# Two hybrid blocks in one kernel: the recurrent pairs and their filler as 64x64 quarters, with "identity minus product" on VectorE

## The reference

```python
def wkv7_scan(r, w, k, v, kk, a, reverse):
    def step(state, inp):
        r_t, w_t, k_t, v_t, kk_t, a_t = inp
        sa = jnp.einsum('bhij,bhj->bhi', state, -kk_t)
        state = (state * w_t[:, :, None, :] + sa[..., None] * (kk_t * a_t)[:, :, None, :]
                 + v_t[..., None] * k_t[:, :, None, :])
        return state, jnp.einsum('bhij,bhj->bhi', state, r_t)
...
    y = direction(0, False) + direction(1, True)      # 8 heads of 64 channels
...
    branch = jnp.einsum('bsnc,ncd->bsnd', ys, w_branch)
    gates = jax.nn.sigmoid(gl.reshape(b, s, N_BRANCH, D_MODEL) + b_gate)
    merged = jnp.sum(gates * branch, axis=2)
```

## Time and profile before

| | |
|---|---|
| median of three runs | 2548.95 us (2546.47 to 2549.86) |
| profiled execution | 2548.45 us, span 2546.7 us |
| granted clock of TensorE, mean | 0.998 |
| PE busy in the span | 2484.2 us, 98% |
| DVE, ACT, POOL busy | 1439.2, 527.6, 316.1 us |

### The profile page before, as it was taken

One profiled execution on the slowest core, in us unless ns is written; L12 is line 12 of the kernel. 1 busy time (PEld: TensorE's weight loads), 2 busy tenths in 40 slices (PEclk: granted clock), 3 DMA queues, 4 the chain that ended last, 5 costly groups with the idle time before them and its releaser, 6 DMA issues. The chain is left out here.

```text
span 2546.7 us, 38463 instructions
## 1 busy us (share of the span) xinstructions
PE 2484.2 (98%) x15968; PEld 1905.6 (75%) x15968; DVE 1439.2 (57%) x2688; ACT 527.6 (21%) x1249; POOL 316.1 (12%) x367
## 2 busy tenths in 40 slices
PE   8999999999999999999999999999999999999998
PEld 7887886854788788685477747888886666666997
DVE  1576655855157655573357735555334488854775
ACT  1342220100134222010014910000003243411000
POOL 2002102110100210221000000000000155410110
PEclk9999999999999999999999999999999999999999
DMA  7331125987433212598632022222222534334553
GB/s 269 116 116 63 57 81 170 303 292 256 147 116 117 68 52 84 179 306 289 239 125 67 2 66 71 96 83 75 91 87 69 165 101 135 121 102 146 167 173 107
DMA packets 253603, 341.80 MB, mean 134 GB/s; under 512 B 7252, under 2 KB 179412, under 8 KB 253304
## 3 DMA queue, kind: packets, MB, share of 16 engines
q1 hardware_dynamic: 241632, 311.71, 37.4%
q10 hardware_dynamic: 8920, 17.67, 2.1%
q0 software_dynamic: 2880, 9.96, 1.0%
HBM read 338.13 MB, written 1.19 MB: 133 GB/s over the span
## 5 line engine op out<-in xcount | busy, mean ns | idle before, releaser
L1058 PE MATMUL PS<-MEM 128*128 128x256 f32 (+1 forms) x2632 | 447.9, 332 | 2.6 <-ACT MEM L1515 1.2
L1058 PEld LDWEIGHTS PS<-MEM 128*128 128x128 f32 x2632 | 406.3, 190 | 43.8 <-issue 1.9
L416 PE MATMUL PS<-MEM 128*128 128x256 f32 x1632 | 356.0, 379 | 0.0
L1474 ACT ACTIVATE MEM<-PS 128x256 f32<-128x256 f32 (+4 forms) x405 | 162.0, 429 | 907.8 <-PE PS L416 221.1
L416 PEld LDWEIGHTS PS<-MEM 128*128 128x128 f32 x1632 | 308.6, 190 | 42.5 <-issue 1.3
L462 PE MATMUL PS<-MEM 128*128 128x512 f32 x608 | 265.4, 597 | 9.1 <-DMA MEM<-w_down 4.3
L2094 DVE SCALAR_TENSOR_TENSOR MEM<-MEM 128x512 f32<-128x512 f32 x280 | 214.4, 798 | 53.7 <-DMA MEM<-ada_w 48.0
L462 PEld LDWEIGHTS PS<-MEM 128*128 128x128 f32 x608 | 115.3, 191 | 155.3 <-issue 141.2
L3038 POOL TENSOR_TENSOR MEM<-MEM 128x1 f32<-128x1 f32 (+1 forms) x34 | 21.6, 637 | 1269.4 <-DVE MEM L2040 812.1
L696 PE MATMUL PS<-MEM 128*128 128x256 f32 x768 | 178.3, 384 | 0.0
L1371 PE MATMUL PS<-MEM 128*128 128x512 f32 (+1 forms) x512 | 171.5, 488 | 0.0
(11 more groups left out here) (384 smaller groups left out, 3259.8 us busy)
## 6 DMA issues: line engine op xcount, KB each, us to landing
MEM<-w_in SPq DMA_DIRECT2D x54, 1024.0 KB, 5.4
MEM<-ada_w SPq DMA_DIRECT2D x48, 1024.0 KB, 7.5
MEM<-w_up SPq DMA_DIRECT2D x32, 1024.0 KB, 5.4
MEM<-w_down SPq DMA_DIRECT2D x32, 1024.0 KB, 5.1
MEM<-ssm_w_in SPq DMA_DIRECT2D x24, 1024.0 KB, 5.4
MEM<-ffn_gate SPq DMA_DIRECT2D x22, 1024.0 KB, 5.3
MEM<-ffn_up SPq DMA_DIRECT2D x22, 1024.0 KB, 5.4
MEM<-ffn_down SPq DMA_DIRECT2D x20, 1024.0 KB, 5.1
```

The source lines that it names most:

```text
L416: ins = pe.matmul(bank[:, 0:T], W[:, k, c * P:(c + 1) * P], XT[:, k, :], start=k == 0, stop=k == KT - 1)
L1058: ins = pe.matmul(out, left[:, k, :], right[:, k, :], start=k == 0, stop=k == 3)
L1474: act.activation(out, view(b), func, **kw).then_inc(S("bank_read_by_act"), 1)
```

## The change

- Every product of the stage but the transposed keys becomes 64x64 (rows x columns of weights). `scores` splits its columns; the right side, the solve and the outputs are split by row half into a first and a second (and third) part, since the second half of the rows adds into the same bank after the first is done, with a semaphore (`row_step`) between them. Quarters of triangular matrices that are zero are left out.
- Filler in this stage runs as pairs of tiles: a step is four 64x64 products of 256 columns over two banks; the first half of a pair's steps takes one row half for each bank, the second the other, with a semaphore (`half_summed`) between.
- VectorE writes identity minus Z instead of ScalarE's copy; X times that is the new X, so ScalarE copies both following products (VectorE one of them at level 5), and VectorE's subtractions go.
- The slots are 2 or 4 steps with the same counts in each pair, their sums end with pairs of tiles; FILL_DECAY is 12 tiles, not 10, and the stage has 112 steps, not 120.
- VectorE reads both states of a pair before both outputs.

```diff
-FILL_LORA, FILL_DECAY, FILL_MEAN, FILL_VAR = 4, 10, 1, 5
+FILL_LORA, FILL_DECAY, FILL_MEAN, FILL_VAR = 4, 12, 1, 5
-FILL_SLOT = {"mask": (4, 0, 0, 0), "begin": (10, 0, 0, 0),
-             ("z", 1): (2, 4, 4, 4), ("z", 2): (0, 0, 0, 0), ("z", 3): (0, 0, 0, 0), ("z", 4): (0, 0, 0, 0), ("z", 5): (4, 4, 4, 4),
-             ("x", 1): (0, 0, 0, 0), ("x", 2): (0, 4, 4, 0), ("x", 3): (0, 0, 0, 0), ("x", 4): (0, 4, 4, 4), ("x", 5): (4, 4, 4, 4),
-             "W": (4, 4, 4, 4), "XO": (2, 2, 2, 4), "sa": (2, 4, 4, 4)}
+FILL_SLOT = {"mask": (4, 0, 0, 0), "begin": (12, 0, 0, 0),
+             ("z", 1): (2,) * 4, ("x", 1): (0,) * 4, ("z", 2): (2,) * 4, ("x", 2): (2,) * 4, ("z", 3): (2,) * 4, ("x", 3): (0,) * 4,
+             ("z", 4): (2,) * 4, ("x", 4): (2,) * 4, ("z", 5): (2,) * 4, ("x", 5): (2,) * 4, "W": (4,) * 4, "XO": (2,) * 4, "sa": (2,) * 4}
...
+                    banks = [bank_for(key, NBANK - 2 + j) for j, key in enumerate(keys)]
+                    for turn in range(2):
+                        if turn:
+                            pe.wait_ge(S("half_summed"), halves[0])
+                        for k in range(nk):
+                            for j, b in enumerate(banks):
+                                r = HB * (j ^ turn)
+                                for o in (0, HB):
+                                    ins = pe.matmul(PS[o:o + HB, b, 0:T], W[r:r + HB, k, (c + j) * P + o:(c + j) * P + o + HB], src[r:r + HB, k, :],
+                                                    start=turn == 0 and k == 0, stop=turn == 1 and k == nk - 1)
...
-                            ins = pe.matmul(banks[half][:, 256 * j:256 * j + 256], BK[pb:pb + 64, d, ct, c, part, :], rhs, start=True, stop=True)
+                            for o in (0, HB):
+                                ins = pe.matmul(banks[half][o:o + HB, 256 * j:256 * j + 256], BK[pb:pb + 64, d, ct, c, part, o:o + HB], rhs, start=True, stop=True)
...
-                        if m in (3, 4):
-                            right_side(gs[m - 3])
                         if m == LEVELS - 1:
                             for g in follow:
                                 keys_flipped(g)
                         slot(pair, ("z", m))
+                        if m == 4:
+                            right_second(gs)
...
+                        if m == 3:
+                            right_first(gs)
                         slot(pair, ("x", m))
                     cross_left(gs)
                     slot(pair, "W")
                     cross_right(gs)
+                    solve_first(gs)
                     slot(pair, "XO")
-                    for g in gs:
-                        solve(g)
+                    solve_second(gs)
+                    outputs_first(gs)
                     slot(pair, "sa")
-                    for g in gs:
-                        outputs(g)
+                    outputs_second(gs)
+                    outputs_third(gs)
...
+                def finer(g):
+
+                    if m < LEVELS - 1:
+                        copy(("dx", l, g, m), flat(UC[g % 2][:, :, :]), lambda b: b[:, 0:256])
+                    elif g % 2 == 0:
+                        b = filled(act, "act", ("dx", l, g, m))
+                        bv = b[:, 0:256].rearrange("p (i n) -> p i n", i=4)
+                        act.activation(AB[g % 4][0:HB, :, 0:HB], bv[0:HB, :, :], ACT.Copy)
+                        act.activation(AB[g % 4][HB:P, :, HB:P], bv[HB:P, :, :], ACT.Copy).then_inc(S("bank_read_by_act"), 1)
...
-                        for g in gs:
-                            copy(("Z", l, g, m), flat(ZI[g % 2][:, :, :]), lambda b: b[:, 0:256])
...
                         slot(("z", m))
+                        if m == 4:
+                            for g in gs:
+                                copy(("rh", l, g), flat(RH[g % 2][:, :, :]), lambda b: b[:, 0:256], scale=-1.0)
+                        for step in (finer_turned, finer) if m == LEVELS - 1 else (finer, finer_turned):
+                            for g in gs:
+                                step(g)
                         slot(("x", m))
...
+                def level_left(g):
+
+                    b = filled(dve, "dve", ("Z", l, g, m))
+                    read(dve.tensor_tensor(ZI[g % 2][:, :, :], eye, b[:, 0:256].rearrange("p (i n) -> p i n", i=4), ALU.subtract))
...
+                        for g in gs:
+                            level_left(g)
                         slot(("z", m))
-                        for step in (finer_turned, finer) if m == LEVELS - 1 else (finer, finer_turned):
-                            for g in gs:
-                                step(g)
+                        if m == LEVELS - 1:
+                            last_diagonal(gs[1])
                         if m in (1, 2):
                             masked("sk", AK, gs[m - 1])
```

More of the change, by code:

```diff
@@ L691, in gate_tiles @@
                         W = a_slab(w_in[l], O_G + D * n + 256 * s)
[L692 to L703, removed]
+                        work = pair_of_tiles([("gl", l, n, 2 * s + c) for c in range(2)], "act", W, 0, XT, KT)
+                        yield from shut(work, 2)
                 def branch_tiles(n, Y):
@@ L708, in branch_tiles, with shut @@
                         W = b_slab(w_branch[l, n], 0, 512 * s)
[L709 to L720, removed]
+                        yield from pair_of_tiles([("br", l, n, 4 * s + c) for c in range(2)], "dve", W, 0, Y, 4)
+                        work = pair_of_tiles([("br", l, n, 4 * s + c) for c in (2, 3)], "dve", W, 2, Y, 4)
+                        yield from shut(work, 2)
+                def shut(work, tiles):
+                    for step in work:
+                        tiles -= step
+                        if tiles == 0:
+                            close_slab()
+                        yield step
                 def gate_work():
@@ L811, in four_blocks @@
                 def four_blocks(gs, keys, by, left, right, halves=(0, HB)):
-                    banks = [take(key, by) for key in keys]
+                    banks = [take(key, who) for key, who in zip(keys, by)]
                     for i in range(4):
@@ L828, in level_z @@
                             emptied(pe, ("dx", l, g, m - 1))
-                    four_blocks(gs, [("Z", l, g, m) for g in gs], "act", lambda g: UM[g % 2][:, m % 2, :, :], lambda g: UC[g % 2])
+                    four_blocks(gs, [("Z", l, g, m) for g in gs], ("dve", "dve"), lambda g: UM[g % 2][:, m % 2, :, :], lambda g: UC[g % 2])
                 def level_x(gs, m):
@@ L872, in cross_right @@
                                 done(ins)
[L874 to L891, removed]
-                                done(ins)
@@ L894, in solve @@
[L894 to L898, removed]
-                    for i in range(4):
[L900 to L917, removed]
-                        ins = pe.matmul(o[i], VTK[:, c, 64 * h:64 * h + 64], AK[i2][:, i, P:2 * P], start=False, stop=wave == 0 and i >= 2)
-                    if wave == 1:
-                        for i, ct, pb, h in inst:
-                            ins = pe.matmul(o[i], ST[pb:pb + 64, d, ct, :], KR[pb:pb + 64, d, ct, c, 1, :], start=False, stop=i >= 2)
-                    done(ins)
@@ new lines, in solve_first @@
+                def solve_first(gs):
+                    for g in gs:
+                        emptied(pe, ("rh", l, g))
+                    open_banks("sa", gs)
+                    for i in range(4):
+                        for g in gs:
+                            for o in (0, HB):
+                                ins = pe.matmul(PS[o:o + HB, opened["sa", g], i * HB:(i + 1) * HB], AB[g % 4][o:o + HB, i, o:o + HB], RH[g % 2][o:o + HB, i, :],
+                                                start=i == 0, stop=i == 3 and o == HB * (g % 2))
+                            if i == 3:
+                                rows_stepped(ins)
@@ new lines, in solve_second @@
+                def solve_second(gs):
+                    for g in gs:
+                        emptied(pe, ("XO", l, g))
+                    other_rows()
+                    for i in range(4):
+                        for g in gs:
+                            f = HB * (g % 2)
+                            r, b = HB - f, opened["sa", g]
+                            ins = pe.matmul(PS[r:r + HB, b, i * HB:(i + 1) * HB], AB[g % 4][f:f + HB, i, r:r + HB], RH[g % 2][f:f + HB, i, :],
+                                            start=False, stop=i == 3)
+                            if i == 3:
+                                numbered(("sa", l, g), "act", b)
+                                done(ins)
@@ new lines, in outputs_first @@
+                def outputs_first(gs):
+                    open_banks("y", gs)
+                    for i in range(4):
+                        for g in gs:
+                            d, c, wave, inst = instances(g)
+                            _, ct, pb, h = inst[i]
+                            f = HB * d
```

(4 more changed lines are left out.)

178 lines of the change are left out of this document (137 added, 41 removed).

## The result

The changed kernel takes 2557.01 us (median of 8 runs, 2552.95 to 2559.38), the kernel before 2549.06 (median of 8 runs in the same comparison; one disturbed run of them, 2891.09, is left out of the ratio). The ratio is 1.0032, 95% interval 1.0023 to 1.0042. It is slower by 0.3%, where 2520 and "faster" were forecast. The profiled execution took 2556.92 us with a span of 2555.1 and a mean granted clock of 0.994.

What follows compares the result with a forecast made beforehand. TensorE, busy 98%, was taken as the bound, with shape changes hidden in "busy". A layer's stage: 3.5 + 10.4 + 112.5 + 14.8 + 1.4 + 1.3 = 143.9 against 158.3; two layers save 28.8, giving 2520 us, range 2499 to 2542.

Steps and rivals of the forecast that it cites:

- Rest: What remains of a layer's stage: 1.4 us for gaps in instruction supply and 1.3 us for the end.
- Theory B: Rival explanation in the experiments: quarters, changes of shape or new waits on VectorE and ScalarE cost more than forecast; no chance given.
- Head: From first scores to first level product: 10.4 us instead of 11.15, as VectorE's queue loses a branch tile.
- steps moved: Eight filler steps (two branch tiles) move ahead of the scores to the decay filler: 3.5 us a layer.
- price of a filler step: Four 64x64 products of 256 columns, four passes at once, take 0.435 us, as one whole product did.
- no loss at a change of shape: With 64x64 products nearly throughout the stage, 110 changes a layer at about 0.16 us, some 17 us, go, all but two round trips.
- The rival in which quarters don't run four at once: Filler passes take turns or pay their weight loads, so the kernel is slower, 2572 or 2604 us; chance 0.06.
- the rule on weight loads: Contrary rule: a load overlaps matmuls in flight only when its row group differs, making a filler step 0.71 us.
- Work and waits of the pairs: TensorE's work in a layer's four pairs, 112.5 us, and its waits there, 14.8 us.
- Supply: Gaps in TensorE's instruction supply, between nothing and 3 us a layer, taken as 1.4.
- The swap of evictions: First product's eviction to VectorE, the two others to ScalarE: no price by itself, both engines answering in 1.1 us.
- I am wrong if ... gaps with no releaser appear by the dozen: Sign against the forecast in the profile after: many TensorE idle gaps that nothing in the profile releases.

Runs made afterwards that it cites:

- whole_filler: The changed kernel with the filler of the pairs as whole 128x128 products again, in the same slots; 2552.18 us, ratio 1.0012.
- slab_pieces: The changed kernel with each weight slab of the stage sent as 8 or 4 DMAs, each held until two more PSUM banks are filled; 2532.05 us, ratio 0.9931.
- pieces_at_once: The changed kernel with the stage's weight slabs sent in 8 or 4 pieces, without waits between the pieces; 2540.6 us, ratio 0.9957.
- slabs_twice: The changed kernel with each weight slab of the stage sent twice, first to a place in DRAM that nothing reads; 2567.79 us, ratio 1.0074.
- pieces_old_evictions: The changed kernel with slabs in pieces and the old evictions: ScalarE copies the first product, VectorE subtracts the two that follow; 2535.69 us, ratio 0.9949.

## Why the prediction was wrong

The step that failed is *Rest*: "Instruction supply ... Bounds: nothing, or a gap in every pair and some (3); I take 1.4." It measured 16.2 and 13.1 us a layer, and the half clock behind it came on top. I had sized it by how often a gap might come, at the 0.3 of the one gap in the earlier trace rows. What sets its length is how late the fetch is, and that was to be read from q8 and q1 in the trace of before: there too no instruction packet comes while a slab runs (271.8 to 275.6: 1021 packets of q1 and none of q8; the next 0.8 us have one). Before, what TensorE had in hand was nearly always enough to bridge that. The number of fetches was to be forecast too: at 250 matmuls and weight loads to a packet, 5120 more are 20 more packets. With 128, 138 and 148 packets (kernel before, whole_filler, changed kernel) the waits without a releaser sum to 0.9, 15.9 and 29.3 us. That the quarters use up sooner what TensorE has in hand fits this; by itself it was not tested, as shapes and slots change along with the count.

The three kernels that move the slabs alone, beside the changed one, account for the loss. Waits and clock are those of the traced execution, so its time stands beside the median. The price of the half clock is an upper bound: 1.7 us for each 3.4 us at 0.50, as the filler block shows (1.77 against 0.86).

| | median, us | traced, us | waits without a releaser, both layers | at half clock in the stages, us |
|---|---|---|---|---|
| slab_pieces | 2532.05 | 2532.66 | 11.6 | 0 |
| pieces_at_once | 2540.6 | 2544.48 | 16.2 | 10.2 |
| changed kernel | 2557.01 | 2556.92 | 29.3 | 20.4 |
| slabs_twice | 2567.79 | 2568.43 | 34.8 | 30.6 |

From slab_pieces to the changed kernel: 17.7 of waits and up to 10.2 of clock, 27.9 for 24.3 between the traced executions; slabs_twice 23.2 and 15.3, 38.5 for 35.8; pieces_at_once 4.6 and 5.1, 9.7 for 11.8, of which a further 3.4 us at half clock outside the stages can hold 1.7. Theory B is not needed for this difference.

The other steps, by slab_pieces, where the supply disturbs least:

- *Head, steps moved, price of a filler step, no loss at a change of shape*: as forecast (in the changed kernel 10.46; the stage starts 3.85 later; 0.43; 0.47). The rival in which quarters don't run four at once is out. So is the rule on weight loads from the Trainium skill ("TensorE: Matmul & The Clock Gate", Part 3), for these products, at 256 columns too: a step takes 0.43, not 0.71.
- *Work and waits of the pairs*: 112.5 + 14.8 = 127.3 forecast. The stage of 146.4 less head 10.5, supply 6.0 and end 1.2 leaves 128.7. The sum came out by luck, as two errors cancel: the trace puts only 5.5 of it down to waits on VectorE and ScalarE, so the work is some 10 longer than I counted block by block, and the waits some 9 shorter. Short waits that the trace doesn't name may be among the work.
- *Supply* is 6.0 and 5.6 even with slabs in pieces, 4.4 a layer over the 1.4. That makes 8.8 of the 12 us by which slab_pieces stays above 2520; 2.8 more are the 1.4 a layer by which work and waits exceed their sum.
- *The swap of evictions* was costed at no price by itself: it costs 4.8 on the kernel before and gains 3.6 with the new slots, most of which can be clock.
- The warning "I am wrong if ... gaps with no releaser appear by the dozen" is what happened: ten in each layer. I had named the symptom and made no rival of it: the 0.06 for "slower" stood for another mechanism.

The Trainium skill has a page on this that I should have weighed ("Runtime: NRT & Kernel Launch", Instruction fetch mechanics): instructions come in blocks of 16 KB over a DMA queue, at a cost that it calls mostly hidden. The size agrees with q8 (2.42 MB in 148 packets); "hidden" holds for the kernel before and not for this one, with 29.3 us.

## What to carry to other kernels

When an edit turns few large products into many small ones, look at how often the instruction queue brings a block, and whether bulk transfers run over the moments at which it must; a short gap with no releaser is a sign that the margin is thin, and no measure of what comes next. A large load that is not urgent is better issued in pieces with work between them: it cost this kernel nothing and turned a loss of 0.3% into a gain of 0.7%. An edit's price can change sign with another (the filler's quarters 4.8 worse or 8.0 better, the swap 4.8 worse or, less surely, 3.6 better), so each is best measured with and without its neighbours.

## What the runs showed of the hardware

- A 16 KB instruction fetch on q8 came behind a 1 MB weight transfer on q1: in the changed kernel never before 84% of the slab's records had begun, and TensorE, which went on 1.2 to 1.6 us after the fetch had landed, stood for up to 4.1 us. With two transfers behind one another it came before the second had ended. It is no law: in whole_filler one fetch came after 45% of a slab (at 967.9), and the 8 KB packets of q14 came in the middle of slabs. The Trainium skill ("DMA: Bandwidth & Descriptors", Queues, rings and completion order) says that a DMA engine changes queues after a packet, typically of 9 to 17 descriptors and at most 64. A slab of the gates is 1040 records here, 65 for each of 16 engines. If such a share went as one packet, that rule would give nearly this, and pieces of 8 records an engine would let a fetch in early; at the typical size, as an estimate, a share would be 4 to 7 packets and a fetch would come in well before the slab's end. The trace doesn't show where packets begin, so this is a reading and not shown.
- Long waits were followed by a slower clock: behind each of the changed kernel's six waits of 2.3 us or more the granted clock fell to 0.50 within 1.5 us of work, and a block of 16 passes took 1.77 instead of 0.86. Behind its waits of 1.7 and 2.0 us, and those of slab_pieces (longest 1.5), it did not in the stage. In slabs_twice it did behind one wait of 2.14 us and not behind one of 2.21, so no border can be read from these runs. The fetch is not needed for it: in pieces_old_evictions two waits of 2.38 us on VectorE were followed by the same.
